# Third attention's scores as three single-pass products of split queries and keys, one chunk later

## What is computed

```
qf = (rms_norm(bcq, g_mla_q[i]) @ w_mla_uq[i]).reshape(b, s_len, 8, 64 + 32)
q_nope, q_pe = qf[..., :64], rope(qf[..., 64:], pos)
kvf = (rms_norm(bckv, g_mla_kv[i]) @ w_mla_ukv[i]).reshape(b, s_len, 8, 64 + 64)
k_nope, vbr = kvf[..., :64], kvf[..., 64:]
k_pe = broadcast_to(rope(bkpe[:, :, None, :], pos), (b, s_len, 8, 32))
s = einsum('bhqd,bhkd->bhqk', concat(q_nope, q_pe), concat(k_nope, k_pe)) * 96 ** -0.5
yb = softmax(where(key's chunk of 64 <= query's, s, NEG_INF)) @ vbr
```

## Time and profile before

| | us |
|---|---|
| median of 3 runs | 1818.25 (1817.81 to 1818.77) |
| profiled execution, its own time | 1818.52 |
| span in that trace | 1816.7 |
| PE busy | 1805.0 (99% of the span) |
| DVE / ACT / POOL busy | 1190.2 / 935.6 / 350.2 |

### The profile page before, as it was taken

The page is one execution under the profiler, slowest core; times in us unless marked ns, Lnnn a source line. Parts: engine busy times, 40 slices in busy tenths (PEclk is TensorE's granted clock), DMA queues, the critical chain, the costliest instruction groups (busy, mean ns, idle before and its releaser), DMA issues.

```text
span 1816.7 us, 26834 instructions
## 1 busy us (share of the span) xinstructions
PE 1805.0 (99%) x9111; PEld 1502.6 (83%) x9111; DVE 1190.2 (66%) x1800; ACT 935.6 (52%) x1660; POOL 350.2 (19%) x314
## 2 busy tenths in 40 slices
PE   9999999999999999999999999999999999999998
PEld 8888888778888888887898888887888888888887
DVE  4756555545477777887656565555455877778874
ACT  4677546533354444455547765465334544445563
POOL 1001001132123333311010020012320234442010
PEclk9999999999999999999999999999999999999999
DMA  6322363579523333685343223544893343336942
GB/s 183 80 83 82 93 123 112 127 180 279 150 67 121 115 116 110 197 307 193 98 145 94 65 82 111 106 130 115 208 282 100 91 120 110 110 118 227 318 139 93
DMA packets 312392, 253.43 MB, mean 140 GB/s; under 512 B 65092, under 2 KB 265440, under 8 KB 312032
## 3 DMA queue, kind: packets, MB, share of 16 engines
q1 hardware_dynamic: 301160, 222.51, 40.5%
q0 software_dynamic: 10752, 29.36, 7.3%
q10 hardware_dynamic: 376, 0.21, 0.1%
HBM read 236.76 MB, written 42.47 MB: 154 GB/s over the span
## 4 chain that ended last, share of the span: by engine, by line
PE 95%; DVE 2%; DMA 1%; ACT 1%; issue 0%; POOL 0%; SPq 0%; DVEq 0%; POOLq 0%; ACTq 0%
PE psum L906 85%; PE psum L1221 2%; PE psum L1187 2%; PE psum L1202 2%; PE psum L949 1%; DMA raw<-in_w_ple_dram 1%; PE psum L1174 1%; PE psum L1173 1%; PE psum L1199 0%; DVE xt L2140 0%; DVE wl L1999 0%; DMA rspill<-rinv_t 0%; PE psum L1184 0%; DVE ydn L2125 0%; PE psum L1413 0%
## 5 line engine op out<-in xcount | busy, mean ns | idle before, releaser
L906 PE MATMUL psum<-xnh,wh 128*128 128x512 f32 (+1 forms) x1424 | 563.8, 396 | 0.3 <-DVE th L2369 0.3
L906 PE MATMUL psum<-xnh,wl 128*128 128x512 f32 (+1 forms) x1424 | 548.5, 385 | 0.0
L906 PE MATMUL psum<-xnl,wh 128*128 128x512 f32 (+1 forms) x1424 | 548.0, 385 | 0.0
L1532 ACT ACTIVATE wh<-raw 128x1024 fp32r<-128x1024 f32 (+2 forms) x276 | 284.6, 1033 | 494.8 <-PE psum L906 458.9
L1999 DVE TENSOR_TENSOR wl<-raw,wh 128x1024 fp32r<-128x1024 f32 (+2 forms) x276 | 365.0, 1324 | 152.4 <-ACT wh L1532 152.0
L906 PEld LDWEIGHTS psum<-xnh,wl 128*128 128x128 f32 x1424 | 267.5, 188 | 54.5
L906 PEld LDWEIGHTS psum<-xnh,wh 128*128 128x128 f32 x1424 | 268.9, 189 | 51.1 <-issue 3.4
L906 PEld LDWEIGHTS psum<-xnl,wh 128*128 128x128 f32 x1424 | 268.2, 188 | 46.6
L2237 DVE CUSTOM_DVE_ANT_0 Sp<-psum,ptok 128x128 f32<-128x128 f32 (+3 forms) x128 | 62.8, 491 | 108.4 <-issue 60.3
L2752 POOL TENSOR_TENSOR merged<-merged,th 128x512 f32<-128x512 f32 x32 | 46.5, 1452 | 266.4 <-DVE th L2369 266.3
L2449 DVE TENSOR_TENSOR ub<-psum,rb 128x512 f32<-128x512 f32 x88 | 60.6, 688 | 39.1 <-PE psum L906 39.1
(11 more groups left out here) (333 smaller groups left out, 3472.4 us busy)
## 6 DMA issues: line engine op xcount, KB each, us to landing
raw<-in_w_up_dram SPq DMA_DIRECT2D x88, 512.0 KB, 3.7
raw<-in_w_gate_dram SPq DMA_DIRECT2D x48, 512.0 KB, 3.8
col_sums<-in_w_down_dram POOLq DMA_DIRECT2D x44, 512.0 KB, 7.9
raw<-in_w_down_dram SPq DMA_DIRECT2D x44, 512.0 KB, 5.0
raw<-in_w_in_dram SPq DMA_DIRECT2D x30, 512.0 KB, 3.7
raw<-col_sums SPq DMA_DIRECT2D x22, 512.0 KB, 4.8
qspill<-f_sums SPq DMA_DIRECT2D x22, 384.0 KB, 4.8
q_raw<-qspill SPq DMA_DIRECT2D x22, 384.0 KB, 6.0
```

Source lines behind the costliest of these rows:

```text
L906: ins = pe.matmul(out, left, right, start=start and n == 0, stop=stop and n == 2)
L1532: act.activation(halves(c)[0][:, 0:n], raw[s][:, 0:n], ACT.Copy).then_inc(w_hi.sem, 1)
```

## The change

The scores of the third attention become three fp32r passes like all other products: high queries by high keys, low by high, high by low. So `qB` becomes `qBh` and `qBl`, `kB` becomes `kBh` and `kBl`.

- **High parts.** ACT's copies of queries and keys now write fp32r. Since an odd head's keys lie in the other half of the partitions, ACT makes them in `Sp` first and copies once more: three activations per pair of heads in place of two. ACT also makes high parts of the turned rope queries (`sq[0]`, `sq[1]`, from `kf`, `acc`; `rope_queries_hi`, after the last `values_out`) and of the rope key (`rx`, from `ytok`).
- **Low parts.** DVE makes `qBl` (`queries_lo`, two operations of 64x512 per bank) straight from PSUM, so DVE releases the bank, not ACT. It makes `kBl` (`keys_lo`, eight operations) and the low rope parts (`rope_parts_lo`, three).
- **Rope rows.** `rope` moves one slot on, behind `lo(ST_LAT+10)`. SP places the sixteen high rows as before, now after `rope_hi`; POOL's queue places sixteen low rows (`rope_low_rows`). The rope key goes out in four broadcasts of 256 KB (high and low, two halves each) in place of two, and they move from `ST_LAT+9` to after the load of `ST_B+4`.
- **One chunk later.** The attention's steps stand in the eleven chunks from `ST_B+1` on, not in the twelve from `ST_B` on.
- **Room.** `qBl` takes `kB`'s place, `kBh` and `kBl` that of finished tiles. The turned probabilities share six tiles in place of twelve. The third attention's output gets tiles of its own over `qBl`, where `xt` comes to lie, so the 2 MB load of `xt` moves from `ST_OUT` to after the load of `ST_OUT+5`.
- **Small ones.** The embedding's `ple_out` is split in two calls in another place; DVE's order in the last attention chunk puts `lo` and `gated` ahead of the steps.

```diff
+KEY_AT = (4, 5, 0, 1, 2, 3, 6, 7)
...
-    qB = here("qB", 0, [P, H, T])
+    qBh = here("qBh", 0, [P, H, T], F32R)
+    qBl = here("qBl", 116, [P, H, T], F32R)
...
-    kB = here("kB", 116, [P, H, T])
+    kBh = here("kBh", 40, [P, H, T], F32R)
+    kBl = here("kBl", 58, [P, H, T], F32R)
...
-            for a, c0, c1 in STAGES + [(2, ST_B, ST_B + 12)]:
+            for a, c0, c1 in STAGES + [(2, ST_B + 1, ST_B + 12)]:
...
-                if c == ST_LAT + 9:
-                    wait(kpe_ready.sem, kpe_ready.at(L, 1))
+                if c == ST_B + 4:
+                    wait(kt_scaled.sem, kt_scaled.at(L, 4))
+                    wait(kpe_hi.sem, kpe_hi.at(L, 1))
+                    wait(kpe_lo.sem, kpe_lo.at(L, 1))
                     for e in range(2):
-                        sp.dma_start(kB[NOPE + HALF * e:NOPE + HALF * e + HALF, :, :],
-                                     ytok[32 * e:32 * e + HALF, :].rearrange("p (o t) -> p o t", o=1
-                                                                             ).to_broadcast([HALF, H, T])
-                                     ).then_inc(kpe_placed.sem, 16)
+                        own = slice(NOPE + HALF * e, NOPE + HALF * e + HALF)
+                        for dst, part in ((kBh, rx), (kBl, ytok)):
+                            sp.dma_start(dst[own, :, :].bitcast(F32),
+                                         part[32 * e:32 * e + HALF, :].rearrange("p (o t) -> p o t", o=1
+                                                                                 ).to_broadcast([HALF, H, T])
+                                         ).then_inc(kpe_placed.sem, 16)
...
-                        wait(rope_sum.sem, rope_sum.at(L, j + 1))
+                        wait(rope_hi.sem, rope_hi.at(L, j + 1))
                     for h in range(H):
                         for e in range(2):
-                            sp.dma_start(qB[NOPE + HALF * e:NOPE + HALF * e + HALF, h, :],
-                                         turned_q[e][HALF * h:HALF * h + HALF, :]
+                            sp.dma_start(qBh[NOPE + HALF * e:NOPE + HALF * e + HALF, h, :].bitcast(F32),
+                                         sq[e][HALF * h:HALF * h + HALF, :]
...
+                if c == ST_OUT + 5:
+                    wait(w_used.sem, w_used.at(L, ST_OUT))
...
-                    pe.wait_ge(kpe_placed.sem, kpe_placed.at(L, 16 * 2))
+                    pe.wait_ge(kpe_placed.sem, kpe_placed.at(L, 16 * 4))
...
-                    pe.wait_ge(kt_empty.sem, kt_empty.at(L, h // 2 + 1))
+                    pe.wait_ge(low_placed[h // 4].sem, low_placed[h // 4].at(L, 16 * 8))
+                    pe.wait_ge(kt_lo.sem, kt_lo.at(L, h // 2 + 1))
...
-                    pe.matmul(o[:, 0:nk(i)], qB[0:NOPE + ROPE, h, P * i:P * i + P], kB[0:NOPE + ROPE, h, 0:nk(i)],
-                              start=True, stop=True).then_inc(s_full.sem, 1)
+                    q_hi_, q_lo_ = (q[0:NOPE + ROPE, h, P * i:P * i + P] for q in (qBh, qBl))
+                    k_hi_, k_lo_ = (k[0:NOPE + ROPE, KEY_AT[h], 0:nk(i)] for k in (kBh, kBl))
+                    pe.matmul(o[:, 0:nk(i)], q_hi_, k_hi_, start=True, stop=False)
+                    pe.matmul(o[:, 0:nk(i)], q_lo_, k_hi_, start=False, stop=False)
+                    pe.matmul(o[:, 0:nk(i)], q_hi_, k_lo_, start=False, stop=True).then_inc(s_full.sem, 1)
...
-            for c in range(ST_B, ST_B + 12):
-                slot(L, c, (2, ST_B, 12))
+            slot(L, ST_B)
+            for c in range(ST_B + 1, ST_B + 12):
+                slot(L, c, (2, ST_B + 1, 11))
...
-                act.activation(qB[0:HD, h, :], b[0:HD, :], ACT.Copy)
-                act.activation(qB[0:HD, h + 1, :], b[HD:P, :], ACT.Copy).then_inc(g_empty.sem, 1)
+                act.activation(qBh[0:HD, h, :], b[0:HD, :], ACT.Copy)
+                act.activation(qBh[0:HD, h + 1, :], b[HD:P, :], ACT.Copy).then_inc(qn_hi.sem, 1)
...
+        def rope_queries_hi(L):
+
+            act.wait_ge(rope_sum.sem, rope_sum.at(L, 2))
+            for e in range(2):
+                act.activation(sq[e][:, :].bitcast(F32R), turned_q[e][:, :], ACT.Copy).then_inc(rope_hi.sem, 1)
...
+            rope_queries_hi(L)
             hi(L, ST_B)
-            for j in range(4):
+            keys_apart(L, 0)
+            hi(L, ST_B + 1)
+            for j in range(1, 4):
                 keys_apart(L, j)
...
+        def queries_lo(L, c, j):
+
+            m = CHUNKS[c][1]
+            h = 4 * m + 2 * j
+            dve.wait_ge(qn_hi.sem, qn_hi.at(L, 2 * m + j + 1))
+            b = G[(G_BASE[c] + j) % 2]
+            for e in range(2):
+                ins = dve.tensor_tensor(qBl[0:HD, h + e, :], b[HD * e:HD * e + HD, :],
+                                        qBh[0:HD, h + e, :].bitcast(F32), ALU.subtract)
+            ins.then_inc(g_empty.sem, 1)
...
+                if c in (ST_LAT + 8, ST_LAT + 9):
+                    queries_lo(L, c - 1, 1)
                 slot(L, c)
                 j = c - ST_LAT - 2
+                if c in (ST_LAT + 7, ST_LAT + 8):
+                    queries_lo(L, c, 0)
...
+                if j == 7:
                     rope(L)
-            for c in range(ST_B, ST_B + 12):
-                slot(L, c, (2, ST_B, 12))
+            rope_parts_lo(L)
...
+        def rope_low_rows(L):
+
+            for j in range(2):
+                pool.wait_ge(rope_lo.sem, rope_lo.at(L, j + 1))
+            for h in range(H):
+                for e in range(2):
+                    pool.dma_start(qBl[NOPE + HALF * e:NOPE + HALF * e + HALF, h, :].bitcast(F32),
+                                   turned_q[e][HALF * h:HALF * h + HALF, :]).then_inc(low_placed[h // 4].sem, 16)
```

More of the change, by code:

```diff
@@ L179, in products_at @@
         return range(0, 2 * H, 2)
-    size = 4 if a == 0 else H
+    size = H if a == 1 else 4
     return range(s - 2 - size, s - 2, 2) if s % size == 2 and s - 2 - size >= 2 * H and s <= STEPS + 2 else ()
@@ L187, in turned_over @@
         return u - 16 if u >= 16 else None
-    packed = 16 if a == 0 else 22
-    if u < packed:
+    if u < 16:
         return None
-    return {0: 3, 1: 7, 2: 9, 3: 11, 4: 13, 5: 15}.get(u - packed, u - (6 if a == 0 else 12))
+    return {0: 3, 1: 7, 2: 9, 3: 11, 4: 13, 5: 15}.get(u - 16, u - 6)
 def windowed(s):
@@ L412, in trunk_kernel @@
     rope_placed = [Tally(sem(f"rope_placed{j}"), 16 * 8) for j in range(2)]
+    low_placed = [Tally(sem(f"low_placed{j}"), 16 * 8) for j in range(2)]
     dve_link = sem("dve_link")
@@ L504, in trunk_kernel @@
     rbkv = here("rbkv", 54, [P, T])
[L505 to L506 removed]
+    yh = [here(f"y{a}h", o, [P, 4, T], F32R) for a, o in enumerate((58, 74, 116))]
+    yl = [here(f"y{a}l", o, [P, 4, T], F32R) for a, o in enumerate((66, 82, 124))]
     kf = here("kf", 90, [P, T])
@@ L513, in trunk_kernel @@
     keys_at = [th[0], th[1], PT[0], PT[1]]
-    PTb = [here(f"PTb{i}", 40 + 2 * i, [P, T]) for i in range(8)]
     def turned_at(a, u):
@@ L524, in turned_at @@
             return tiles[2 + (u - 8) // 2][:, 2 * P * (u % 2):2 * P * (u % 2) + 2 * P]
-        return tiles[(u - 16) % 6 if a == 0 else (u - 10) % 12][:, :]
+        return tiles[(u - 16) % 6][:, :]
     ytok = here("ytok", 108, [P, T])
@@ L1697, in post, with ple_out @@
                     act.activation(mh[:, mm, :], merged[:, mm, :], ACT.Copy, scale=0.5).then_inc(m_hi.sem, 1)
-        def ple_out(L, c):
+        def ple_out(L, c, tiles=range(TB)):
             m = CHUNKS[c][1]
-            for t in range(TB):
+            for t in tiles:
                 if t < TB - 1:
@@ L2228, in attention @@
                     dve.wait_ge(rq_ready.sem, rq_ready.at(L, 1))
+                if s < 2 and a == 2:
+                    dve.wait_ge(kt_lo.sem, kt_lo.at(L, 4))
                 if s == 0 and a == 0:
@@ L2490, in slot @@
             soon = [s for k in range(FIRST_LO) for s in att_steps(att[2], c - att[1], k)] if steps else []
+            ends = att is not None and att[0] == 2 and c == att[1] + att[2] - 1
+            if ends:
+                lo(L, c + 1)
             for s in soon:
@@ L2493, in slot @@
                     attention(L, att[0], s)
-            if kind != "ukn":
+            if ends:
+                gated(L, c, 0)
+            elif kind != "ukn":
                 lo(L, c + 1)
+            if last == "ukn":
+                for j in range(4):
+                    keys_lo(L, j)
             if last in ("kA", "qA"):
@@ L2500, in slot @@
                 attention(L, att[0], s)
-            if kind[:6] == "branch":
+            if kind[:6] == "branch" and not ends:
                 gated(L, c, 0)
```

67 lines of the change are left out of this document (53 added, 14 removed).

## The result

The change made the kernel slower: 1861.13 us (median of four, 1859.91 to 1862.37) against 1818.51, a ratio of 1.0235 (1.0217 to 1.0253), 42.6 us. I had forecast 1846 with a range to 1858. The sign and the place were right; the size of its largest term was not. The profiled execution took 1862.08 us, with a span of 1860.3.

What follows compares the result with a forecast made beforehand. The prediction took PE, busy 99% of the span, as the bound. Per layer 1.4 + 1.4 + 11.2 + 1.6 - 1.9 = 13.7 us, two layers 27.4, raised 1818.5 to a forecast of 1846 us, range 1833 to 1858.

Steps and rivals of the forecast that it cites:

- its largest term: PE standing before the third attention's first score until the rope key's broadcasts land: 11.2 us per layer.
- Scores: Third attention's scores as three fp32r passes: 2.16 us per head becomes 1.92, a gain of 1.9 us per layer.
- First and second wait: PE waits at the sums of the keys' latent and in ukv for uqn1's second bank: 1.4 us each per layer.
- the long wait: PE's stand before the third attention's first score, for the rope key's broadcasts: forecast 11.2 us per layer.
- Third wait: Before the third attention's step 0, PE waits for four rope-key broadcasts, last landing at 308.8: 11.2 us per layer (6.6 to 15.2).
- the far end: Latest landing forecast for the last rope-key broadcast, one behind the other at 2.7 us pitch: 312.8 us.
- Clock: PE's clock falls to half rate after the idle time before the third attention: 1.6 us per layer, at most 5.4.
- At nothing: Terms priced at zero: ACT's and DVE's added copies, forty steps in eleven chunks, the xt load; low rope rows nothing, at worst 1 us.
- the first rival: SP's sixteen rope-row issues cost nothing, broadcasts land by 302.1, PE waits 4.5 us: 1832 us in total; chance 0.09.
- The wait is dearer: Rival: four broadcasts one behind the other, lower clock for a chunk or longer, low rows late: 1858 to 1866 us; chance 0.10.

Runs made afterwards that it cites:

- the last version: Changed kernel with early kBl broadcasts, rope rows shared with POOL, attention from ST_B+3, sums' add first, spread_scale earlier, last key pair later: 1816.71 us, ratio 0.9994.
- the short-wait run: Kernel before the change with four added DVE operations ahead of the second zkvl and the add into sq, so PE waits at the sums: 1825.77 us, ratio 1.0040.

## Why the prediction was right or wrong

*Scores, right.* The chain's pieces after, second pass at 128, 256, 384 and 512 keys (start us, us, what), against the earlier trace rows:

```profile
321.89 0.11 PE psum L1205
...
333.52 0.12 PE psum L1205
...
354.12 0.17 PE psum L1205
...
377.82 0.23 PE psum L1205
```

Counted from start to start over the first layer, the 32 scores took 17.12 us before and 15.26 in the last version: 1.9 us, as forecast. I missed that the products with the values now come in groups of four heads, not eight: counted alike, transposes and products take 16.5 us, not 15.7, so 0.8 of it goes back.

*First and second wait, right in size, wrong in price.* 1.3 and 1.05 us by PE's rows for 1.4 and 1.4. But I put the lower clock on the long wait alone. The first wait, too, brings it down, at 1.65 us, in some layers; the short-wait run shows that by itself.

*Third wait, the step that failed: "I take 6.6 for the last of four, so 308.8".* Up to SP's first broadcast the working held: it left at 301.3 for 300.2, and 1.4 us of that had come in the execution's first 20 us. From there two sizes were wrong. I let the four broadcasts leave 0.67 us apart; the third issue took 2.98 us, and the last left 4.6 us behind the first, not 2.0. And it took 9.71 us to land, not 6.6, so at 315.6. Even the far end, 312.8, was too near, for two reasons the runs separate. The broadcasts carry 1 MB at 104 to 118 GB/s, 2.0 to 2.5 us each on full DMA engines. In the kernel before, the two had moved no faster:

```profile
256.00:258.00 2.00, 2.00 (x11) 1.65 (x10) 1.50 (x3) 0.39 (x1) 0.00 (x0) 1.00 0.91 108
```

So their 4.6 and 6.6 us held the price of one and of two transfers, not a delay that several could share. And what stands ahead of them on the same engines delays the first one: it landed 8.3 us after its issue, not 4.6, behind 1 MB of gates and the last of the low rows (ahead of the loads 5.0). I took a latency from a row and should have taken a rate: bytes by GB/s, summed over all that is queued. An estimate that way: 1 MB at 339 GB/s and 1 MB at 115, from 302 on, end at 314.2. Counted by when PE's next matmul would have started, the wait is 16.5 us in the first layer instead of 11.2, and 17.2 in the second.

*Clock, right in kind, low in size.* 1.6 taken; 5.3 and 5.0 us at 0.50 measured, worth 1.4 to 2.65 us a layer.

*At nothing, wrong twice.* `ple_out`, which I left out of the sum, gives back 1.3 us a layer by the traces, 1 us by the times; that is luck, for the forecast has no word on it. PE never waited for the low rows themselves, as said, but by sharing the DMA engines they make the long wait 1.15 us a layer longer by the traces, 1.7 by the times; that is part of the third wait's size. `xt` cost nothing, as said.

*The sum.* Per layer, from the second: 1.3 and 1.65 (sums and clock), 1.1 (bank), 17.2, 2.5 (clock), less 1.9 and 1.3, plus 0.8: 21.3 us. The first has 19.0, without the clock's first fall. That is 40.3 of the 43.6 us between the spans; 1.4 more lie in the profiled execution's first 20 us, which vary from run to run, 0.8 in a wait for `dn_lh` at 861 us that several other runs show too (0.5 to 0.7), and 1.1 I can't assign. The long clock is taken at its upper price. The far end of the forecast's own sum, 1861, meets the measured time by luck: its wait is too short, and its 5.4 us for the clock are twice what came.

*The rivals.* The cheap issue of the first rival is neither right nor wrong: eight rows fewer on SP gave 2.5 us a layer where 5.0 of issue went. The Trainium skill, DMA: Bandwidth & Descriptors, "Issuing engines are not separate DMA queues", has the other half, that all queues end on the same sixteen engines. The run with eight rows on POOL's queue agrees: the last broadcast then took 12.05 us to land instead of 9.71. "The wait is dearer" came true by its first cause, the broadcasts one behind the other; the clock was low for about a chunk's time, at half of its price. It had a chance of 0.10 because I trusted one row's latency.

## What to carry over

Price a transfer that you add or move by its rate in the stretch where it lands and by all bytes queued on the DMA engines ahead of it, not by the issue-to-landing time of a lone one; the broadcasts here ran at a third of a load's rate. Cover for such a transfer must be sought on the DMA engines as well: a later start alone gave back 31 of the 42.6 us and moved part of the wait to the weights behind the broadcasts; sending half of the broadcasts earlier, into an idle stretch, together with a later start, removed it. And a wait of little more than a microsecond next to small matmuls can cost twice its length, when the clock falls behind it.
